# Layer 1's weight slabs: 512 columns by half of the contraction instead of 256 columns by all of it, and eight diagonals in rotation instead of four

## The reference, cut to what matters

```
def odd_layer(x, ...):                       # the mixer of layer 1
    proj = rmsnorm(x, norm_mix) @ w_in       # 1024 x (1352 + 1024)
    p_c, p_d = proj[..., :C_COLS], proj[..., C_COLS:]
    o_c, k, v, kidx = dsa_mixer(p_c, ...)    # attention over selected keys
    o_d, d_v = gmlp_mixer(p_d, ...)
    x = x + concatenate([o_c, o_d]) @ w_out  # 1024 x 1024

def peer_ffn(x, w_q, keys, u_tab, v_tab):
    q = x @ w_q                              # 1024 x 1024
    ...                                      # top 16 x 16 keys of each head
    ue, ve = u_tab[eidx], v_tab[eidx]        # gathered rows
    h = gelu(einsum('td,thkd->thk', xb, ue))
    return einsum('thk,thkd->td', gate * h, ve)
```

## Time and profile before

| | us |
|---|---|
| median of 3 runs | 4042.57 (4039.16 to 4043.38) |
| the profiled execution, its time | 4045.94 |
| its span, first to last instruction | 4044.2 |
| TensorE busy | 3189.1 (79%) |
| VectorE busy | 2664.7 (66%) |
| ScalarE busy | 1348.9 (33%) |
| GpSimd busy | 1382.6 (34%) |

### The profile page before, as it was taken

How to read it: one execution, slowest core, us unless ns; L and a number is a source line. 1 busy time by engine, 2 the same in 40 slices (tenths; PEclk the granted TensorE clock), 3 DMA queues, 4 the chain that set the end, 5 groups by cost and what they waited for, 6 DMA issues and landing times.

```text
span 4044.2 us, 35286 instructions
## 1 busy us (share of the span) xinstructions
PE 3189.1 (79%) x10090; PEld 1660.9 (41%) x10090; DVE 2664.7 (66%) x6448; ACT 1348.9 (33%) x4000; POOL 1382.6 (34%) x1218
## 2 busy tenths in 40 slices
PE   8865499787776777778998877789897887777777
PEld 4444389543332332245544542454344422222222
DVE  0088555226667666676899767679986767667665
ACT  1144122013333333232367323224552323333332
POOL 0021000013444444343443444344344434444443
PEclk9887599799999999998998989989999999999999
DMA  3100000247999999999999999999999999999998
GB/s 126 36 1 6 0 1 1 69 144 309 421 422 421 419 418 408 422 402 359 367 389 345 401 354 421 384 353 421 360 410 419 419 403 422 421 421 420 418 419 355
DMA packets 229842, 1284.84 MB, mean 318 GB/s; under 512 B 23568, under 2 KB 73744, under 8 KB 82064
## 3 DMA queue, kind: packets, MB, share of 16 engines
q0 software_dynamic: 165888, 1208.03, 73.2%
q1 hardware_dynamic: 63760, 74.57, 5.5%
HBM read 1278.12 MB, written 3.87 MB: 317 GB/s over the span
## 4 chain that ended last, share of the span: by engine, by line
DMA 37%; PE 24%; DVE 9%; issue 6%; ACT 3%; POOL 0%; DVEq 0%; ACTq 0%; POOLq 0%; SPq 0%
DMA ring<-in_uv,route 30%; PE banks L1505 16%; DMA own<-in_l_w_in 5%; DVE ring L1445 4%; PE banks L1826 2%; PE banks L2312 2%; DMA own<-in_l_w_out 1%; PE banks L1884 1%; ACT route L1490 1%; PE banks L1877 1%; DVE X L1455 1%; DVE own L2130 1%; DMA own<-in_l_peer_wq 1%; ACT route L1475 1%; PE banks L1851 0%
## 5 line engine op out<-in xcount | busy, mean ns | idle before, releaser
L1505 PE MATMUL banks<-ring,route 128*128 128x512 f32 (+1 forms) x4224 | 2033.8, 619 | 533.5 <-ACT route L1490 526.2
L1445 DVE SCALAR_TENSOR_TENSOR ring<-ring,XN 128x1024 f32<-128x1024 f32 x1152 | 1409.1, 1223 | 771.3 <-DMA ring<-in_uv,route 766.7
L1434 POOL DMA_INDIRECT ring<-in_uv,route x1152 | 1286.9, 1117 | 1823.9 <-PE banks L1505 1648.0
L1505 PEld LDWEIGHTS banks<-ring,route 128*128 128x128 f32 (+1 forms) x4224 | 751.4, 188 | 1602.3 <-issue 829.4
L1475 ACT ACTIVATE route<-route 128x2 f32<-128x2 f32 x576 | 117.2, 203 | 1697.7 <-DVE ring L1445 1697.2
L1490 ACT ACTIVATE route<-IDN,route 128x128 f32<-128x128 f32 x928 | 318.9, 386 | 3.1 <-PE banks L1505 2.5
L1480 ACT ACTIVATE route<-route 128x1 f32<-128x1 f32 x1152 | 276.8, 287 | 23.2
L1826 PE MATMUL banks<-own,QP 128*128 128x225 f32 (+2 forms) x800 | 187.6, 378 | 71.4 <-DMA own<-in_l_w_in 71.4
L1826 PEld LDWEIGHTS banks<-own,QP 128*128 128x128 f32 x800 | 158.3, 199 | 127.0 <-issue 118.7
L111 POOL TENSOR_TENSOR ys<-ys,IDN 128x4 f32<-128x4 f32 x9 | 9.1, 1008 | 389.1 <-DVE ys L1188 389.1
L1455 DVE SCALAR_TENSOR_TENSOR X<-ring,route,X 128x1024 f32<-128x1024 f32 x96 | 123.0, 1281 | 21.9 <-ACT route L1480 21.0
(11 more groups left out here) (411 smaller groups left out, 3359.8 us busy)
## 6 DMA issues: line engine op xcount, KB each, us to landing
ring<-in_uv,route POOLq DMA_INDIRECT x1152
own<-in_l_peer_wq SPq DMA_DIRECT2D x9, 1024.0 KB, 24.7
own<-in_l_w_in SPq DMA_DIRECT2D x8, 1024.0 KB, 25.8
own<-in_l_w_out SPq DMA_DIRECT2D x8, 1024.0 KB, 25.1
own<-in_l_w_in SPq DMA_DIRECT2D x8, 900.0 KB, 26.1
W<-in_l_w_in SPq DMA_DIRECT2D x2, 2560.0 KB, 21.4
X<-in_x_prompt SPq DMA_DIRECT2D x8, 512.0 KB, 8.4
WO<-in_l_w_out SPq DMA_DIRECT2D x4, 1024.0 KB, 8.9
```

Source lines behind the costliest of these rows:

```text
L1434: pool.indirect_dma_start(self.ring[:, s % RING, :], None, self.io[f"uv{of_slot(s)[0]}"], bass.IndirectOffsetOnAxis(ap=self.EI[:, g % 2, k ...
L1445: dve.scalar_tensor_tensor(u, u, 1.0, self.XN[:, of_slot(s)[1], :], ALU.mult, ALU.mult, accum_out=self.HD[:, g % 2, k:k + 1]).then_inc(sel ...
L1505: m = pe.matmul(self.bank[1 + half][0:n, :], self.DG[:, (V_TENSOR[s] - 1) % 4, 0:n], self.ring[:, s % RING, D + 512 * half:D + 512 * half ...
```

## The change

Columns are taken 512 at a time (`COLUMNS`: 0, 512, 1024 to 1352, then two of 512), and each such group is loaded in two slabs: slab 2g holds the first 512 rows of the contraction (`HK` = 4 pieces of 128), slab 2g + 1 the other 512. A slab has the same bytes as before (1 MB; 656 KB for the 328 columns). TensorE adds up the first half for all tiles, each in a bank of its own, then the second half in the same banks; so a product is complete only at the end of every second slab. Banks rotate over five instead of three. The end of an even slab is told by a semaphore of its own, `half_slabs`. Slabs, buffers and due times in slots stay in number: half as many matmuls, twice as wide, are spread over the same slots. In the queries the matmuls keep their shape, and four heads are open at once. `DG` has eight entries instead of four.

```diff
-        self.DG = take([4, P])
+        self.DG = take([8, P])
...
-            if n >= 4:
-                act.wait_ge(self.v_tensor.h, n - 3)
-            act.activation(self.DG[:, n % 4, 0:cols], on, ACT.Copy,
+            if n >= 8:
+                act.wait_ge(self.v_tensor.h, n - 7)
+            act.activation(self.DG[:, n % 8, 0:cols], on, ACT.Copy,
...
-SLABS = [(0, 226), (226, 452), (452, 677), (677, 902), (902, 1127), (1127, CCOLS)] + [
-    (CCOLS + 256 * i, CCOLS + 256 * i + 256) for i in range(4)]
+COLUMNS = [(0, 512), (512, 1024), (1024, CCOLS), (CCOLS, CCOLS + DW), (CCOLS + DW, CCOLS + 2 * DW)]
 NC, ND, NO, NQ = 6, 4, 4, 4
+HK = KD // 2
...
         for s in range(NC + ND):
             for i in range(nt):
                 n = s * nt + i
-                for k in range(KD):
-                    pe.append((10 + (n + k / KD) * c, "in", n, k))
-                act.append((10 + (n + 1) * c + 2, "project", n))
+                for k in range(HK):
+                    pe.append((10 + (n + k / HK) * c, "in", s // 2, i, HK * (s % 2) + k))
+                if s % 2:
+                    act.append((10 + (n + 1) * c + 2, "project", s // 2, i))
...
-        for h in range(PH):
-            for k in range(KD):
-                pe.append((query + (h + k / KD) * q, "query", h, k))
-            act.append((query + (h + 1) * q + 2, "query", h))
+        for j in range(NQ):
+            for i in range(4):
+                n = 4 * j + i
+                for k in range(HK):
+                    pe.append((query + (n + k / HK) * q / 2, "query", j // 2, i, HK * (j % 2) + k))
+                if j % 2:
+                    act.append((query + (n + 1) * q / 2 + 2, "query", 4 * (j // 2) + i))
...
-        pick = {"turn": lambda w, i, b: 3 + (2 * i + b) % 4, "in": lambda n, k: 5 + n % 3, "mix": lambda i: 7, "heads": lambda i, b: 3 + (5 * i + b) % 2,
+        pick = {"turn": lambda w, i, b: 3 + (2 * i + b) % 4, "in": lambda g, i, k: 3 + (g * nt + i) % 5, "mix": lambda i: 7, "heads": lambda i, b: 3 + (5 * i + b) % 2,
...
-    def slab_end(self, s):
+    def slab_end(self, eng, s):
 
         if s < 0:
-            return self.before.slab_end(s + NC + ND + NO + NQ)
...
+            self.before.slab_end(eng, s + NC + ND + NO + NQ)
+        elif s % 2 == 0:
+            eng.wait_ge(self.hs_.h, self.hs_.at(s // 2 + 1))
+        elif s < NC + ND:
+            self.banks.get(eng, self.at["in", s // 2, self.nt - 1])
...
-            sp.dma_start(to, w[:, :, i:j]).then_inc((self.sl0, self.sl1)[s % 2].h, 16)
+            to = self.W[s % 2][:, 0:HK * (j - i)].rearrange("p (k n) -> p k n", k=HK)
+            sp.dma_start(to, w[:, HK * (s % 2):HK * (s % 2) + HK, i:j]).then_inc((self.sl0, self.sl1)[s % 2].h, 16)
...
-            m = pe.matmul(out[:, 0:W.shape[2]], self.QP[:, self.tiles[i], k, :], W[:, k, :],
+            m = pe.matmul(out[:, 0:W.shape[2]], self.QP[:, self.tiles[i], k, :], W[:, k % HK, :],
                           start=(k == 0), stop=(k == KD - 1))
+            part_end = i == nt - 1
...
         if kind not in ("in", "out", "query") or k == KD - 1:
             b.filled(m, at)
+        elif k == HK - 1 and part_end:
+            m.then_inc(self.hs_.h, 1)
```

More of the change, by code:

```diff
@@ L1504, in pe_weigh @@
         for half in range(2):
-            m = pe.matmul(self.bank[1 + half][0:n, :], self.DG[:, (V_TENSOR[s] - 1) % 4, 0:n],
+            m = pe.matmul(self.bank[1 + half][0:n, :], self.DG[:, (V_TENSOR[s] - 1) % 8, 0:n],
                           self.ring[:, s % RING, D + 512 * half:D + 512 * half + 512],
@@ L1719, in plan @@
                 self.at[kind, *place] = self.banks.claim(pick[kind](*key))
-    def slab_end(self, s):
+    def slab_end(self, eng, s):
         if s < 0:
-            return self.before.slab_end(s + NC + ND + NO + NQ)
[L1725 to L1730, removed]
+            self.before.slab_end(eng, s + NC + ND + NO + NQ)
[3 more added lines that the diff above has]
+            self.banks.get(eng, self.at["in", s // 2, self.nt - 1])
+        elif s < NC + ND + NO:
+            self.banks.get(eng, self.at["out", (s - NC - ND) // 2, self.nt - 1])
+        else:
+            self.banks.get(eng, self.at["query", (s - NC - ND - NO) // 2, 3])
     def slab(self, pe, s):
@@ L1820, in pe @@
         elif kind == "in":
-            n, i = key[0], key[0] % nt
-            W = self.slab(pe, n // nt)
-            if n < nt and k == 0:
+            g, i, k = key
+            W = self.slab(pe, 2 * g + k // HK)
+            if g == 0 and k == 0:
                 for half in range(2):
                     b.spent(pe, self.at["turn", 0, i, half])
-            m = pe.matmul(out[:, 0:W.shape[2]], self.QP[:, self.tiles[i], k, :], W[:, k, :],
+            m = pe.matmul(out[:, 0:W.shape[2]], self.QP[:, self.tiles[i], k, :], W[:, k % HK, :],
                           start=(k == 0), stop=(k == KD - 1))
+            part_end = i == nt - 1
         elif kind == "mix":
@@ L1871, in pe @@
         elif kind == "out":
-            n, i = key[0], key[0] % nt
-            W = self.slab(pe, NC + ND + n // nt)
-            if n < nt and k == 0:
+            g, i, k = key
+            W = self.slab(pe, NC + ND + 2 * g + k // HK)
+            if g == 0 and k == 0:
                 for half in range(2):
                     b.spent(pe, self.at["out_turn", i, half])
-            m = pe.matmul(out[:, 0:256], self.QP[:, self.tiles[i], k, :], W[:, k, :], start=(k == 0), stop=(k == KD - 1))
-        else:
-            h = key[0]
-            W = self.slab(pe, NC + ND + NO + h // 2)
-            if h == 0 and k == 0:
+            m = pe.matmul(out, self.QP[:, self.tiles[i], k, :], W[:, k % HK, :], start=(k == 0), stop=(k == KD - 1))
+            part_end = i == nt - 1
+        else:
+            g, i, k = key
+            W = self.slab(pe, NC + ND + NO + 2 * g + k // HK)
+            if g == 0 and i == 0 and k == 0:
                 for half in range(2):
                     b.spent(pe, self.at["turn", 1, nt - 1, half])
-            m = pe.matmul(out[:, 0:self.width()], W[:, k, 128 * (h % 2):128 * (h % 2) + 128], self.XQ[:, k, 0:self.width()],
+            m = pe.matmul(out[:, 0:self.width()], W[:, k % HK, i * P:i * P + P], self.XQ[:, k, 0:self.width()],
                           start=(k == 0), stop=(k == KD - 1))
+            part_end = i == 3
         if kind not in ("in", "out", "query") or k == KD - 1:
             b.filled(m, at)
+        elif k == HK - 1 and part_end:
+            m.then_inc(self.hs_.h, 1)
     def width(self):
@@ L1900, in act @@
             else:
-                b.spent(act, self.at["out", (NO - 1) * nt + i])
+                b.spent(act, self.at["out", 1, i])
             act.activation(self.XN[:, t, :], self.X[:, t, :], ACT.Square,
@@ L1972, in act @@
             h, = key
-            src = b.get(act, self.at["query", h])
+            src = b.get(act, self.at["query", h // 4, h % 4])
             f = self.tiles[0]
@@ L1980, in act @@
                 ins = act.activation(self.QP[:, 4, h, a:a + DEC], src[:, 2 * P:2 * P + DEC], ACT.Copy)
-            b.empty(ins, self.at["query", h])
+            b.empty(ins, self.at["query", h // 4, h % 4])
     def pool(self, pool, kind, *key):
@@ L2009, in before @@
             dve.wait_ge(self.steps.h, ch.n)
-        self.banks.spent(dve, self.at["in", (NC - 1) * self.nt + i])
+        self.banks.spent(dve, self.at["in", NC // 2 - 1, i])
         before()
@@ L2060, in settle @@
         dve.wait_ge(self.ll.h, self.ll.at(32))
-        self.banks.spent(dve, self.at["in", (NC + ND - 1) * self.nt + i])
+        self.banks.spent(dve, self.at["in", (NC + ND) // 2 - 1, i])
         ch.add(dve.tensor_reduce(mean, v, AX.X, ALU.add))
@@ L2333, in _ @@
                     if h == 0 and j in q_pass:
-                        banks.spent(pe, q_pass[j].at["query", PH - 1])
+                        banks.spent(pe, q_pass[j].at["query", 1, 3])
                         if q_pass[j] is one:
```

45 lines of the change are left out of this document (21 added, 24 removed).

## The result

The changed kernel takes 3991.23 us (median of 4 runs, 3988.4 to 3992.14), the kernel before, beside it, 4040.86 (4033.72 to 4043.38). The ratio is 0.9879, 95% interval 0.9862 to 0.9896: 1.2% faster, at least 1.0%. The profiled execution took 3988.4 us.

What follows compares the result with a forecast made beforehand. Transfers bound the kernel, except where TensorE's slab waits let them run dry. Gains of 25, 22, 2 and 7 us sum to 56, less 3 for VectorE: 53 off 4042.57 gives 3990, range 3965 to 4034.

Steps and rivals of the forecast that it cites:

- What bounds the kernel: Steady stretch: transfers set the pace, DMA share 1.01 at 418 GB/s, 2.52 us a slot; the ring of 8 hides the rest.
- The waits make the rate fall: Layer 1's mixers: TensorE waits 105.3 us for slabs, frees no ring entry, gathers stop and DMA engines run dry.
- A landing goes by its number of packets, taken in turn: Slab loads beside gathers: 32 packet pairs of 0.379 us per engine plus 5.7, so 17.8 us to land instead of 26.
- A's input projection, 25 us: Mixer A's input projection: slabs land within 20.4 us each, so the rate recovers from 372 to 418 GB/s; 25 us gained.
- B's, 22: Mixer B's input projection: slabs land just in time at 18.1 us each; 22 us gained.
- A's output and queries, 9: Mixer A's output part gains 2 us; its queries gain 7, with a wait of 5.9 us left instead of 12.8.
- B's output and queries, 0: Mixer B's output and queries: no wait left, but waits there cost nothing before; gain 0.
- VectorE is late next, minus 3: Right behind A's slabs, 1980 to 2060 us: VectorE busy 76.9 of 80, so work arriving sooner queues; 3 us taken off.
- TensorE gains nothing from width: Slab matmuls: 0.90 and 0.92 ns a column at either width, so wider instructions alone give TensorE 0.
- Diagonals, 0: ScalarE's diagonals: eight in rotation can return at most the 2.5 us ACT waited for TensorE; counted as 0.
- The rivals: Slab loads: landings don't shrink (4042, chance 0.08), slower (4052, 0.08), or only part of the gain (4015, 0.18).
- The slower rival: Slab loads: turns bounded near 1 KB, so 2 KB rows take two; 9 us more, 4052; chance 0.08.

Runs made afterwards that it cites:

- before_diag8: The kernel before with eight diagonals in rotation instead of four and nothing else; 4042.21 us, ratio to before 0.9991 to 1.0012.
- rows_1k: The changed kernel with each slab fetched by two DMAs of half the columns, so 1024 packets of 1 KB again; 4040.47 us.
- tuned_b: The changed kernel with mixer B's second-tile search, attention, output and queries spread over spare slots, VectorE's shares moved along; 3984.55 us.
- quarter_1k: The changed kernel with slabs of a quarter of the contraction in four half-size buffers, and rows of 1 KB; 3999.59 us.
- after_noload: The changed kernel without slab loads except each mixer's first two, so results are not the reference's; 3921.4 us.
- quarter: The changed kernel with slabs of a quarter of the contraction in four half-size buffers, rows still 2 KB; 3993.33 us.

## Why the prediction was right

I forecast 3990 with a range of 3965 to 4034; 3991.23 was measured. That it came within 1.2 us is in part luck. The forecast was a gain of 53 us from a median of 4042.57; the kernel before, timed beside the changed one, took 4040.86, so the gain is 49.6. Between the two profiled executions it is larger, 4045.94 to 3988.4 or 57.5 us, and all the stages below are of these two: their gains add up to 70.9 us against my 56, and what is lost elsewhere to some 13 against my 3. Stages of single executions also scatter: in `before_diag8`, which is the kernel before but for its diagonals, the two input projections took 3.6 us less and 3.0 more than before.

- *What bounds the kernel.* The transfers, but for the mixers: this rests, as argued, on the share of 1.01 and 1.02 at 418 to 421 GB/s in the steady stretch and, now, in both projections; no run changed the gathers. Both kernels without loads reach the same 3921 us, so the slabs' loads are what sets the two apart.
- *The waits make the rate fall.* Shown: `rows_1k` brings back the waits and the time together, at the lower rate. That a stop came only at every second slab I had read off but not explained. The trace of before fits this: when TensorE has stood and the gathers run dry, the next slab has the engines almost to itself. TensorE stood until 1864.95, and from 1868 to 1872 SP's queue finished 731 packets and the gathers' 87.
- *A landing goes by its number of packets, taken in turn.* Shown three times: by the one to one counts at 656 B, 900 B, 1 KB and 2 KB, by `rows_1k`, and by the slabs of 656 KB below, whose 512 packets take as long to land as the 512 of a megabyte. In the trace of before the counts stay equal in each 2 us from 1796 to 1822 too (95 to 106 against 95 to 104), so a turn isn't many rows. I said 17.8 us to land; measured are 16.1 and 16.8, in the page of `tuned_b`, whose loads are the changed kernel's (the page of the latter gives no landing for them): DMA issues, KB each, median us to landing.

```profile
own<-in_l_w_in SPq DMA_DIRECT2D x16, 1024.0 KB, 16.1
...
own<-in_l_w_out SPq DMA_DIRECT2D x8, 1024.0 KB, 16.8
...
own<-in_l_w_in SPq DMA_DIRECT2D x4, 656.0 KB, 16.1
```

  My term was too large in the pair: 0.353 us, not 0.379. A 2 KB packet took 24.0% of 16 engines over 10 us for 453, or 0.085 us, not the 0.096 of the earlier trace rows, where such loads alone were moving; a gather's took 78.1% for 454, or 0.275, not 0.283. (Added up they give 0.360: the shares come to 102%, so a sum of prices is a little over the pair, in the earlier trace rows as well.) So 32 x 0.353 = 11.3 us are turns, and about 4.8 lie outside.
- *A's input projection, 25 us.* By the timeline of GpSimd, gathers 334 to 404 went out in 223.6 us before and in 196.7 now: 26.9. In `rows_1k` it was 212.3, but a stop of 12.5 us stands right behind; up to gather 410 the times are 239.5 before, 213.1 now, 237.7 in `rows_1k` and 218.9 in `quarter_1k`.
- *B's, 22.* Gathers 590 to 650: 197.1 to 170.0, 27.1. Mis-sized by 5: I had priced a slab at 3.0 us on top of its slots, which made 18.1 us a slab and 3.0 a slot; measured are 17.0 and 2.83 (170.0 us for ten slabs and 60 slots), and the loads cost 2.2 a slab over the whole (from `after_noload`).
- *A's output and queries, 9.* Gathers 492 to 580: 265.2 to 253.3, 11.9. The wait left in A's queries was to be 5.9 us; it is 3.97 and a second one of 1.06.
- *B's output and queries, 0.* Gathers 770 to 848: 221.8 to 216.8, so 5.0 us less; but just ahead of it, gathers 760 to 770 took 2.7 more, and in `quarter`, with no wait at all, 770 to 848 took 222.2. That waits there were nearly free held.
- *VectorE is late next, minus 3.* It was 4.5 behind A's projection (gathers 404 to 432: 73.9 to 78.3), where VectorE is busy 78.23 of 80 us in 1940 to 2020, at 396 GB/s; the pair without loads, which comes there sooner still, took 78.3 and 79.4. Another 5.0 were lost behind B's (650 to 672: 55.5 to 60.5), which I had left out, and 3.5 from 672 to 770, the 2.7 above among them; what holds the gathers back there no run shows. The two errors, gains too small and losses too small, went opposite ways, and the close hit owes to that.
- *TensorE gains nothing from width.* Shown by the pair without loads: 0.5 us apart, and the input projections keep TensorE busy for 176.0 us in 800 instructions before and for 176.3 in 400 now. With the stops, both are near 188 (the pages of before and of `rows_1k`), so the lower busy time of the changed kernel, 176.2, goes with the stops and their lower clock, not with the width. The groups of the pair without loads, of before and of `rows_1k`:

```profile
L1828 PE MATMUL banks<-own,QP 128*128 128x225 f32 (+2 forms) x800 | 176.0, 364 | 0.0
L1835 PE MATMUL banks<-own,QP 128*128 128x512 f32 (+1 forms) x400 | 176.3, 566 | 2.2 <-ACT QP L1926 2.2
L1826 PE MATMUL banks<-own,QP 128*128 128x225 f32 (+2 forms) x800 | 187.6, 378 | 71.4 <-DMA own<-in_l_w_in 71.4
L1836 PE MATMUL banks<-own,QP 128*128 128x512 f32 (+1 forms) x400 | 188.1, 594 | 67.1 <-DMA own<-in_l_w_in 64.9 <-ACT QP L1927 2.2
```

- *Diagonals, 0.* Shown.
- *The rivals.* The Trainium skill ("DMA: Bandwidth & Descriptors", Specifications) has 512 B as enough for full rate, which for the rate alone this trace hardly contradicts: 2 KB in 0.085 us against 1 KB in 0.045 (14.4% of 16 engines over 10 us for 510 in `rows_1k`) is 6% better. But rate was not what the wider rows bought; it was turns, and rows of 1 KB gain nothing over those of before (`rows_1k`). The slower rival, a turn of bounded bytes, is refuted up to 2 KB; its sum counts 34 slabs where the two mixers load 36, which changes it by less than 1 us.

## What to carry to other kernels

When a load shares the DMA engines with a queue that is always full of larger packets, ask how many packets it has, not how many bytes: its landing is (packets for each engine) x (one packet of each queue), and here some 5 us on top. Make rows longer by cutting the other dimension, here the contraction, with partial sums kept in spare PSUM banks; or, if that can't be, start the load earlier with more and smaller buffers, which gave 41 of 49 us. Price a wait by what it lets run dry: 12 us of waits in B's output and queries cost at most some 5, the 71 us in the input projections 54 (between the two profiled executions).

## What the runs showed of the hardware

- A megabyte slab's landing was 25 to 26 us with 1024 packets and 16 to 17 us with 512, beside gathers of 8 KB rows; with 512 packets, 656 KB took the same 16.1 us as 1 MB.
- A 2 KB packet cost 0.096 us where only such loads were running and 0.085 us between gathers' packets.
- The input projections' matmuls, 400 instructions of up to 512 columns or 800 of up to 256, kept TensorE busy equally long (176.3 and 176.0 us in the pair without loads).
